# Expert weights copied as bf16 in more places and in separate rows, gate and up products over the widest bucket only

## The reference

```python
h = h + mixer(rmsnorm(h))            # causal pooling (4 windows) beside RWKV-7 (16 heads of 64, a scan over 2048 tokens)
h = h + memory_xattn(rmsnorm(h))     # 4 heads, 256 memory tokens
# hierarchical MoE: one of 4 groups, in it 2 of 4 experts
g_idx = argmax(t @ w_group + b_group)
top_v, top_i = top_k((t @ w_expert + b_expert)[group g_idx], 2)
for e in range(16):
    hid = silu(t @ w_gate[e]) * (t @ w_up[e])       # 2048 -> 512, twice
    out = out + gates[:, e] * (hid @ w_down[e])     # 512 -> 2048
return rmsnorm(h + out)
```

## Time and profile before

| | |
|---|---|
| time, median of 3 runs | 2512.99 us (2512.98 to 2514.11) |
| the profiled execution's own time | 2513.94 us |
| its span on the slowest core (core 5) | 2512.3 us |
| spans of cores 0 to 7 | 2507.9, 2497.2, 2505.5, 2495.1, 2497.2, 2512.3, 2502.6, 2504.0 us |
| TensorE busy, mean granted clock of core 5 | 2277.4 us (91%), 0.957 |
| DVE, ACT, POOL busy | 1384.6, 1238.9, 393.5 us |
| DMA queue of POOL (q0), of SP (q1) | 217.45 MB, 151.64 MB |

### The profile page before, as it was taken

The page is one execution under the profiler, slowest core; times in us unless marked ns, Lnnn a source line. Parts: engine busy times, 40 slices in busy tenths (PEclk is TensorE's granted clock), DMA queues, the critical chain, the costliest instruction groups (busy, mean ns, idle before and its releaser), DMA issues.

```text
span 2512.3 us, 57398 instructions; the slowest of 8 cores (2495.1 to 2512.3 us)
## 1 busy us (share of the span) xinstructions
PE 2277.4 (91%) x25144; PEld 1280.5 (51%) x25144; DVE 1384.6 (55%) x2599; ACT 1238.9 (49%) x2303; POOL 393.5 (16%) x655
## 2 busy tenths in 40 slices
PE   5789999899788899999997999999994999999986
PEld 2355555554455555554554555555552555555543
DVE  3455666677636567676774334343435555666644
ACT  5555776677656676676774323233332232433312
POOL 3122113111130212211000000000001012111111
PEclk9989999999889999999997999999996999999998
DMA  9768567664883868965466676767765788999973
GB/s 217 98 108 119 93 108 108 110 114 80 143 126 94 116 114 126 136 113 96 88 138 171 160 137 152 146 154 145 152 124 187 178 242 224 243 241 258 251 210 114
DMA packets 183805, 372.80 MB, mean 148 GB/s; under 512 B 80992, under 2 KB 134752, under 8 KB 169856
## 3 DMA queue, kind: packets, MB, share of 16 engines
q0 software_dynamic: 100560, 217.45, 52.5%
q1 hardware_dynamic: 82992, 151.64, 18.9%
HBM read 510.79 MB, written 121.77 MB: 252 GB/s over the span
## 4 chain that ended last, share of the span: by engine, by line
PE 77%; DMA 11%; DVE 5%; ACT 4%; issue 2%; POOL 1%; POOLq 0%; DVEq 0%
PE ps L128 77%; ACT big L151 4%; DMA big<-w_lo 3%; DVE big L158 3%; DVE big L163 2%; DMA big<-w_kv 1%; DMA big<-x 1%; DMA big<-wg_l 1%; DMA out<-big 1%; DMA big<-w_qT 1%; DMA qkd<-big 1%; POOL big L193 1%; DMA big<-h_s,big 1%; DMA big<-mem 1%; DMA vod<-big 0%
## 5 line engine op out<-in xcount | busy, mean ns | idle before, releaser
L128 PE MATMUL ps<-big 64*64 64x64 bf16 (+6 forms) x25144 | 2277.4, 262 | 212.0 <-ACT big L151 68.3
L128 PEld LDWEIGHTS ps<-big 64*64 64x64 bf16 (+3 forms) x25144 | 1280.5, 109 | 1208.4 <-issue 147.5
L151 ACT ACTIVATE big<-ps 128x512 bf16<-128x512 f32 (+2 forms) x904 | 505.7, 588 | 810.8 <-PE ps L128 794.7
L158 DVE TENSOR_TENSOR big<-ps,big 128x512 bf16<-128x512 f32 (+3 forms) x656 | 465.4, 721 | 439.8 <-PE ps L128 312.1
L151 ACT ACTIVATE big<-big 128x512 f32<-128x512 f32 (+9 forms) x896 | 541.2, 634 | 256.6 <-DVE big L158 107.3
L151 ACT ACTIVATE big<-ps,big 128x512 f32<-128x512 f32 (+3 forms) x332 | 211.4, 649 | 184.8 <-PE ps L128 181.4
L163 DVE SCALAR_TENSOR_TENSOR big<-ps,big 128x512 f32<-128x512 f32 (+2 forms) x316 | 223.6, 721 | 138.3 <-ACT big L151 83.6
L163 DVE SCALAR_TENSOR_TENSOR big<-big 128x512 bf16<-128x512 f32 (+4 forms) x212 | 227.7, 1078 | 35.3 <-DMA big<-h_s,big 19.2
L158 DVE TENSOR_TENSOR big<-big 128x512 bf16<-128x512 f32 (+11 forms) x406 | 200.2, 511 | 30.2 <-ACT big L151 24.2
L163 DVE SCALAR_TENSOR_TENSOR big<-big,ps 128x64 f32<-128x64 f32 (+1 forms) x280 | 92.6, 331 | 168.3 <-PE ps L128 166.3
L179 DVE CAST big<-ps 128x512 bf16<-128x512 f32 x168 | 110.8, 684 | 60.2 <-ACT big L151 45.1
(11 more groups left out here) (27 smaller groups left out, 309.8 us busy)
## 6 DMA issues: line engine op xcount, KB each, us to landing
big<-x SPq DMA_DIRECT2D x32, 1024.0 KB, 7.5
big<-w_rkv POOLq DMA_DIRECT2D x48, 512.0 KB, 8.9
wuc<-wu_l POOLq DMA_DIRECT2D x40, 512.0 KB, 7.5
wgc<-wg_l POOLq DMA_DIRECT2D x40, 512.0 KB, 7.4
wdc<-wd_l POOLq DMA_DIRECT2D x40, 512.0 KB, 7.3
big<-wuc SPq DMA_DIRECT2D x40, 512.0 KB, 9.7
big<-wgc SPq DMA_DIRECT2D x40, 512.0 KB, 7.5
big<-wdc SPq DMA_DIRECT2D x40, 512.0 KB, 8.9
```

Source lines behind the costliest of these rows:

```text
L128: r.append(e.matmul(out, lhsT=lhsT, rhs=rhs, start=st, stop=sp_, **k))
L151: return self.op("act", lambda e: e.activation(out=out, in_=in_, func=func, **kw), dur, R, W, P, tbl=TBL.get(func))
L158: return self.op(eng, lambda e: e.tensor_tensor(out=out, in0=a, in1=b, op=op), dur, R, W, P, after=after)
```

## The change

Five things change.

1. The scratch `wec` gets rows of 2112 values of which 2048 are used, so that its rows no longer follow each other without a gap, and a piece can't be merged into longer stretches.
2. `EXM, ERC = 18, 36`: 144 pieces are recast instead of 120, 72 in the first stage instead of 56, 72 in the second instead of 64. 48 are left to come as float32 in the expert stage, instead of 72.
3. The gate and up matmuls number 1 to 14 of the 16 of a sum take their column shape from a register: 3 buckets of `nm` columns with a step of 128, where `nm` is the largest count among the expert's three buckets (at least 1, at most 128). The first and the last of the 16 still run over all 384. Eight small DVE operations compute the 16 values `nm` from `run`; ahead of the second bucket's transposes, PE loads them into registers and writes 16 shape registers with four instructions.
4. In `st_chain` the output matmuls of two chunks (`YB = 2`) are issued as one operation.
5. The planner: a successor on PE is ready as soon as its predecessor ends, without the 255 ns; a float32 matmul with a tile position counts 0.52 instead of 2.06 ns a column; the gate and up matmuls count as 300 columns.

```diff
-                r = o.end + (LAT if not o.bytes else 0.0)
+                r = c + d if e == "pe" and s.eng == "pe" else o.end + (LAT if not o.bytes else 0.0)
...
-            if lhsT.dtype == F32 and not (len(it) > 5 and it[5].get("is_transpose")):
-                dur += 2.06 * n
+            if lhsT.dtype == F32 and not kw5.get("is_transpose"):
+                dur += (0.52 if "tile_position" in kw5 else 2.06) * n
...
+                if "shape" in k:
+                    k.pop("cols")
+                    sr = k.pop("shape")
+                    out, rhs = out.shape_from_register(sr), rhs.shape_from_register(sr)
                 r.append(e.matmul(out, lhsT=lhsT, rhs=rhs, start=st, stop=sp_, **k))
...
-EXM, ERC = 14, 30
+EXM, ERC = 18, 36
...
+YB = 2
...
-    wec = [dint(n, [16, 4, 128, 2048]) for n in ("wgc", "wuc", "wdc")]
+    wec = [dint(n, [16, 4, 128, 2112])[:, :, :, 0:2048] for n in ("wgc", "wuc", "wdc")]
...
+                ys_.append((c, Sp))
+                if c % YB == YB - 1:
+                    it = []
+                    for c_, Sq in ys_:
+                        g = []
...
+                    S.mm(it, R=[AR, NB, KB, TV] + [Sq for _, Sq in ys_ if Sq], P=[bky])
+                    ys_ = []
...
+            r6 = r3(run.a, 4)
+            n4 = r3(nmx.a, 4)
+            S.red(n4[:, :, 0], r6[:, :, 0:3], ALU.max, R=[run], P=[nmx])
+            for i, (a, b, c) in ((1, (0, 3, 4)), (2, (1, 3, 5)), (3, (2, 4, 5))):
+                S.tt(n4[:, :, i], r6[:, :, a], r6[:, :, b], ALU.max, R=[run], P=[nmx])
+                S.tt(n4[:, :, i], n4[:, :, i], r6[:, :, c], ALU.max, R=[run, nmx], P=[nmx])
+            S.ts(nmi.a, nmx.a, 128.0, ALU.min, 1.0, ALU.max, R=[nmx], W=[nmi])
...
+                r = [e.load(regs, nmi.a[0:1, :])]
+                for rg, v in ((one, 1), (w128, 128), (three, 3)):
+                    e.reg_mov(rg, v)
+                for i in range(0, 16, 4):
+                    r.append(e.move_shape([e.shape_register(j) for j in range(i, i + 4)], [[(one, regs[j]), (w128, three), (one, one), (one, one)] for j in range(i, i + 4)]))
...
-                        S.group([([(pp.a[:, 0:384], w3[:, kc, :], X3[:, kc, :], kc == 0, kc == 15) for kc in range(8 * kk, 8 * kk + 8)], [w, XE[e]]) for kk in range(2)], pp)
+                        sh = dict(shape=nc.tensor.shape_register(e), cols=300)
+                        S.group([([(r3(pp.a[:, 0:384], 3), w3[:, kc, :], r3(X3[:, kc, :], 3), kc == 0, kc == 15, sh if kc % 15 else {}) for kc in range(8 * kk, 8 * kk + 8)],
+                                  [w, XE[e], shp]) for kk in range(2)], pp)
```

More of the change, by code:

```diff
@@ L850, in st_chain @@
                     S.stt(Z.a, chain["Z"].a, chain["G"][0], cza, ALU.mult, ALU.add, R=[chain["Z"], chain["G"][1], bkc], W=[Z])
-                it = []
-                for h in range(2):
-                    y = Y3[HS[h], c, :]
-                    if Sp is not None:
-                        it.append((y, Sp.a[HS[h], :], A3[HS[h], c, 64:128], True, False))
-                    it.append((y, K3[HS[h], c, 0:64], N3[HS[h], c, 64:128], Sp is None, False))
-                    it.append((y, V3[HS[h], c, :], K3[HS[h], c, 64:128], False, True))
-                it = [it[i] for i in ((0, 3, 1, 4, 2, 5) if Sp is not None else (0, 2, 1, 3))]
-                S.mm(it, R=[AR, NB, KB, TV] + ([Sp] if Sp else []), P=[bky])
+                ys_.append((c, Sp))
[3 more added lines that the diff above has]
+                        g = []
+                        for h in range(2):
+                            y = Y3[HS[h], c_, :]
+                            if Sq is not None:
+                                g.append((y, Sq.a[HS[h], :], A3[HS[h], c_, 64:128], True, False))
+                            g.append((y, K3[HS[h], c_, 0:64], N3[HS[h], c_, 64:128], Sq is None, False))
+                            g.append((y, V3[HS[h], c_, :], K3[HS[h], c_, 64:128], False, True))
+                        it += [g[i] for i in ((0, 3, 1, 4, 2, 5) if Sq is not None else (0, 2, 1, 3))]
+                    S.mm(it, R=[AR, NB, KB, TV] + [Sq for _, Sq in ys_ if Sq], P=[bky])
+                    ys_ = []
                 marks.append(S.ops[-1])
@@ L1246, in build, with shapes @@
             S.cp(flgi.a, flg.a, R=[flg], W=[flgi])
+            r6 = r3(run.a, 4)
[5 more added lines that the diff above has]
+            S.ts(nmi.a, nmx.a, 128.0, ALU.min, 1.0, ALU.max, R=[nmx], W=[nmi])
+            shp = Buf()
+            def shapes(e):
+                regs = [es.enter_context(e.register(f"nm{i}")) for i in range(16)]
+                one, w128, three = [es.enter_context(e.register(n)) for n in ("c1", "c128", "c3")]
+                r = [e.load(regs, nmi.a[0:1, :])]
[3 more added lines that the diff above has]
+                    r.append(e.move_shape([e.shape_register(j) for j in range(i, i + 4)], [[(one, regs[j]), (w128, three), (one, one), (one, one)] for j in range(i, i + 4)]))
+                return r
             wxr = Ring([S.part(o_, 1024) for o_ in WP[:12]])
@@ L1289, in gather @@
                     S.mm([(pb.a[:, j * 128:(j + 1) * 128], xn.a[:, (q * 4 + j) * 128:(q * 4 + j + 1) * 128], identb.a, True, True) for j in range(4)],
-                         R=[xn, identb], W=[pb])
+                         R=[xn, identb] + ([nmi] if (b, q) == (1, 0) else []), W=[pb] + ([shp] if (b, q) == (1, 0) else []), pre=shapes if (b, q) == (1, 0) else None)
                     for k in range(2):
@@ L1409, in build @@
             nc.all_engine_barrier()
+    mybir.codegen_inst_isa_subclasses(nc)
     return nc
```

15 lines of the change are left out of this document (9 added, 6 removed).

## The result

The changed kernel takes 2480.74 us (median of 4 runs, 2476.17 to 2487.17) against 2513.55 us for the kernel before on the same chip: ratio 0.987, 95% interval 0.9846 to 0.9894. That is 33 us faster. I had forecast 64 us, with 2449 inside a range of 2415 to 2500. The direction and the mechanism held; half of the gain did not come.

What follows compares the result with a forecast made beforehand. PE was taken to set the pace, with DMA not far behind: 2513.9 - 75 (columns) + 1 (registers) + 12 (weights) + 4 (recasts) - 6 (order) = 2450, predicted as 2449 us against the runs' median; range 2415 to 2500.

Steps and rivals of the forecast that it cites:

- Gate and up products: Expert stage: 1792 shaped matmuls cost only their columns, 76.7 us less on core 5, 68.5 on core 2; term -75 us.
- rival 3: Expert stage: shaped matmuls bound by their own issue, 176 ns each whatever their columns; total 2536 us; chance 0.14.
- The weight stream: Expert stage: DMA share rises to 0.93 in a shorter dense stretch, so PE sometimes waits for weights; +12 us, between 0 and 25.
- rival 1: Expert stage: weights set the pace, DMA holds its 0.88 share and PE waits; total 2470 us; chance 0.14.
- a fallen clock in the expert stage: Expert stage: sign that the forecast is wrong altogether, PE idling between shorter matmuls; no size given.
- The register load: Start of the expert stage: PE's load of 16 registers and four shape instructions stays covered by DVE's norm; +1 us, between 0 and 4.
- The recast pieces in the first stage: First stage: 16 more recast pieces delay loads sharing POOL's queue; +4 us, between 0 and 26.
- rival 2: First stage gets longer: recast pieces delay loads (+26) and the new order falls worse (+10); total 2487 us; chance 0.09.
- The new order: First stage: 34 fewer tile mode changes (-3 us) and a reshuffled plan; -6 us in all, -35 to +20 held possible.

## Why the prediction was right in direction and too large

**Gate and up products: right.** The term was 76.7 us of columns for core 5 and 68.5 for core 2. At a clock of 1.00 shaped matmuls are 121 ns apart on core 5 and 126.5 on core 2 at the mean, which makes 74 and 65 us; core 7 has 69. A shaped matmul is spaced by its columns (93 to 155 ns by expert), so rival 3, 176 ns whatever the columns, is out.

**The weight stream: the step that failed.** I took +12 us for waits. On core 7 the idle time rose by 12.6 us (26.0 to 38.6), just that; that it is so near is in part luck, since I got it by weighing two bounds. What the term left out is that PE pays for such a wait twice: behind the one shown the clock is at 0.50. Over the stage PE was busy 61.7 us less where the columns alone are 69: some 7 us went to the clock against the kernel before, and 12.2 against the run without float32 loads. Columns, idle time and clock together make 69 - 12.6 - 7.3 = 49.1, which is the difference of the two windows. The stage's gain of 51 us (median) is that of rival 1, "the gain of the stage is 75 - 25 = 50", to which I had given 0.14. Its reason was half right. DMA did hold its share (0.84; 0.86 before), but the share is not the limit: without float32 loads the engines carry more at 0.77, and PE hardly waits, and with 32 of them, all gate pieces, PE hardly waits at 0.84. What the traces show of the float32 loads is that each takes twice the engines' time of a recast piece, in the bursts in which scatters and gathers fall, and that pieces of both queues, scatters and gathers land late there. They also stand ahead of gathers in POOL's queue; on core 7 PE's wait for a gather so held up is 1.08 us (issued at 2373.4 us), and on four other cores such a wait is 1.7 to 3.7 us. So this is the smaller part; how the 30 us divide was not measured. I had seen a 22.38 us float32 load on the chain and set it aside, because PE's waits on weights were 0.3 us. The run with shapes alone, with its 29.9 us, shows that these were small because PE was slow.

I had named "a fallen clock in the expert stage" as what would make the prediction wrong altogether, and priced it at nothing. It fell by two hundredths against the kernel before, for 7 us.

**The register load: the overlap failed.** +1 us predicted, 5.0 measured. I counted 25 sequencer steps of 0.06 us, all covered by the wait for DVE's norm. The load is one instruction of 4.01 us, about 0.25 us a register, and it comes behind that wait and not under it, because it carries the same wait itself. The Trainium skill (Runtime: NRT & Kernel Launch, Instruction fetch mechanics) gives about 200 ns a register; the trace agrees roughly, with 0.25 us.

**The recast pieces in the first stage: near.** +4 us predicted within 0 to 26. On the cores without the stretch at 0.81 the 16 pieces cost 16 to 20 us under the old plan (two cores), but some 6 under the new one (pooled medians 1381 for 72 and 1375 for 56). Beyond 72 pieces the price is higher: 17 us for the next 8, 24 for 16 and 74 for 48, that is 1.5 to 2 us a piece; below, 48 pieces gain nothing. The wait on w_kv, by which I sized the term, rose by only 5 us:

```profile
PE ps L133 <- ACT big L156: 73.7, 50, 22.5
...
PE ps L133 <- DMA big<-w_kv: 15.9, 13, 3.2
```

The wait on ACT rose by 7. That a late load delays an activation, and PE's wait is then put down to ACT, fits this, and was not shown. In the second stage nothing was lost, as forecast. The sign that I gave for rival 2, a second stage that starts after 1375 us, was of no use: I had put the end of the first stage at 1359 us, but on core 5 of the kernel before its last 64x64 matmul ends at 1379.1.

**The new order: not told from nothing.** -6 us predicted; some -2 by the table for the costs alone. The outputs of two chunks together (YB) were not run alone. With the recast pieces the first stage came out 8 us longer in the pair of traces above and 4 by the pooled medians, where I had -2; that these two terms came out small was within what I had held possible, and no run shows why.

**What adds up.** Of the 31 us that are missing, 12 lie in the expert stage (51 in place of 63), 4 in the register load and 10 in the first stage of the two executions traced (6 by the pooled medians); the rest is which core is the slowest. By the ratios, the shapes alone give -13 us and the recast pieces alone +18; and the costs alone some -3 on the cores whose mean clock is 0.956 or more. Together they give -33. The expert stage is where they do not add: shapes alone -21, recast pieces alone -8, both -51. Fewer float32 loads are worth little while PE is the bound, and shorter products are worth little while the loads are; each part makes room for the other. Taken out of the changed kernel, the recast pieces cost 18 us in the expert stage and give back some 6 to 11 in the first: the net of 0.987 against 0.991 lies within the intervals. None of the splits tried beats the changed kernel by more than its interval.

## What to carry to other kernels

When the bounding engine's work is cut, price the next resource twice: the idle time, and the slower clock in which PE works after each idle stretch. Look for the next bound not in the mean share of a resource but in its bursts and in queues whose entries stand behind each other; here one run that replaced 48 loads of one kind showed the 30 us that a share of 0.84 hid. Cost two parts that work on the same stage together, since alone each shows only what the other lets through. Look up what a small setup instruction waits for before counting it as covered: here it shared an operation, and so a wait, with the work it was to hide behind. And before two executions are compared by the times of a stage, compare the granted clock in it, core by core.

## What was not expected of the hardware

- Packets of 4 KB in place of 32 KB stretches for recast pieces changed nothing in the time (0.987 against 0.9871).
- A load of registers on PE's queue takes about 0.25 us a register (1.20 us for 4, 2.89 for 12, 4.01 for 16).
- The granted clock was 0.81 from about 100 to 264 us on some cores, in executions of the kernel before as of the others, which makes the first stage some 16 us longer at the median.
- Five kernels end later after their last matmul: 27.5 to 31.6 us in place of 23 to 24 (recast pieces alone, no float32 loads, 80, 88 and 120 pieces in the first stage). The time is that of POOL's drain behind the last scatter, 5.5 to 10.1 us in these and 1.8 to 2.7 in the others; what makes it long is open.
